# Transposing the residual's first half one weight part later, in a two-layer hybrid encoder step on one core

## The reference, cut to what matters

```
z = rmsnorm(h, ln_in) @ w_in                      # split: attention, gates, convolution
y_a = rmsnorm(o_a * silu(g_a), ln_out_a)          # 512 columns, from attention
y_c = rmsnorm(v * silu(g_c), ln_out_c)            # 512 columns, from the convolution
h = h + concatenate([y_a, y_c]) @ w_out           # (1024 x 1024)
gate = sigmoid(rmsnorm(h, ln_pg) @ w_pg)          # (1024 x 1024)
h = h + gate * (p @ w_pe)
```

## Time and profile before

| | us |
|---|---|
| median of 3 runs | 846.02 |
| lowest and highest | 844.46, 846.97 |
| the profiled execution, its time | 844.46 |
| the profiled execution, its span | 842.6 |
| PE busy in the span | 785.6 (93%) |
| DVE busy | 572.4 (68%) |
| ACT busy | 410.5 (49%) |

### The profile page before, as it was taken

How to read it: one execution, slowest core, us unless ns; L and a number is a source line. 1 busy time by engine, 2 the same in 40 slices (tenths; PEclk the granted TensorE clock), 3 DMA queues, 4 the chain that set the end, 5 groups by cost and what they waited for, 6 DMA issues and landing times.

```text
span 842.6 us, 10488 instructions
## 1 busy us (share of the span) xinstructions
PE 785.6 (93%) x3782; PEld 608.4 (72%) x3782; DVE 572.4 (68%) x1093; ACT 410.5 (49%) x944; POOL 67.9 (8%) x104
## 2 busy tenths in 40 slices
PE   6999999889998899999999999998999889999992
PEld 5789778547665568888888878774667556888881
DVE  3337968878894786555463688788899577656455
ACT  3655645544345573244365474555343547223544
POOL 5000123000000340000000012220000011000000
PEclk9999999989999999999999999999999999999996
DMA  9622222110000053412172223120000003342203
GB/s 298 186 71 76 70 66 79 35 51 4 22 26 1 25 184 111 154 63 90 51 263 66 75 70 89 46 69 26 26 26 25 1 1 106 133 137 75 76 1 124
DMA packets 40569, 65.26 MB, mean 77 GB/s; under 512 B 7774, under 2 KB 19898, under 8 KB 40502
## 3 DMA queue, kind: packets, MB, share of 16 engines
q1 hardware_dynamic: 37354, 58.45, 21.7%
q0 software_dynamic: 3104, 6.12, 2.5%
q10 hardware_dynamic: 60, 0.02, 0.0%
HBM read 57.86 MB, written 7.17 MB: 77 GB/s over the span
## 4 chain that ended last, share of the span: by engine, by line
PE 84%; ACT 8%; DVE 4%; issue 2%; DMA 1%; SPq 0%; DVEq 0%; ACTq 0%
PE acc L598 18%; PE acc L600 18%; PE acc L599 17%; PE sharedT L532 6%; PE sharedS L802 4%; PE acc L711 4%; PE sharedO L814 4%; PE sharedT L791 3%; ACT JUNK L928 2%; PE sharedT L785 2%; PE sharedO L532 1%; PE sharedS L532 1%; ACT WHI L932 1%; ACT KH L932 1%; PE sharedS L751 1%
## 5 line engine op out<-in xcount | busy, mean ns | idle before, releaser
L598 PE MATMUL acc<-WHI,XHI 128*128 128x512 f32 (+1 forms) x720 | 310.5, 431 | 3.0 <-DVE WLO L1285 2.3
L600 PE MATMUL acc<-WHI,XLO 128*128 128x512 f32 (+1 forms) x720 | 279.9, 389 | 0.0
L599 PE MATMUL acc<-WLO,XHI 128*128 128x512 f32 (+1 forms) x720 | 279.2, 388 | 0.0
L1349 DVE SCALAR_TENSOR_TENSOR VT<-UX,CWT,VT 128x640 f32<-128x640 f32 x240 | 211.9, 883 | 5.3
L1285 DVE SCALAR_TENSOR_TENSOR WLO<-WR,GT,WHI 128x512 fp32r<-128x512 f32 (+1 forms) x144 | 100.1, 737 | 103.9 <-ACT WHI L932 103.8
L598 PEld LDWEIGHTS acc<-WHI,XHI 128*128 128x128 f32 x720 | 136.4, 189 | 33.4 <-issue 6.0
L599 PEld LDWEIGHTS acc<-WLO,XHI 128*128 128x128 f32 x720 | 136.5, 190 | 28.9 <-issue 6.0
L600 PEld LDWEIGHTS acc<-WHI,XLO 128*128 128x128 f32 x720 | 135.8, 189 | 26.8
L932 ACT ACTIVATE WHI<-WR,GT 128x512 fp32r<-128x512 f32 (+1 forms) x144 | 94.8, 708 | 114.1 <-PE acc L600 108.7
L932 ACT ACTIVATE PT<-sharedT 128x384 f32<-128x384 f32 (+1 forms) x80 | 35.9, 449 | 76.3 <-PE sharedT L532 76.1
L814 PEld LDWEIGHTS sharedO<-V,PT 128*128 128x128 f32 x320 | 44.2, 191 | 19.6 <-issue 14.5
(11 more groups left out here) (191 smaller groups left out, 855.8 us busy)
## 6 DMA issues: line engine op xcount, KB each, us to landing
WR<-in_w_in_dram SPq DMA_DIRECT2D x32, 256.0 KB, 3.1
WR<-in_w_in_dram SPq DMA_DIRECT2D x16, 512.0 KB, 3.6
WR<-in_w_out_dram SPq DMA_DIRECT2D x16, 512.0 KB, 3.8
WR<-in_w_pg_dram SPq DMA_DIRECT2D x16, 512.0 KB, 3.5
WR<-in_w_in_dram SPq DMA_DIRECT2D x8, 416.0 KB, 3.4
residual_spill<-H SPq DMA_DIRECT2D x5, 512.0 KB, 3.4
H<-residual_spill SPq DMA_DIRECT2D x10, 256.0 KB, 3.2
H<-in_x_prompt_dram SPq DMA_DIRECT2D x4, 512.0 KB, 8.1
```

The costliest lines, as they stand in the source:

```text
L598: mm(out, hi, w_hi, start=(first and k == 0), stop=False)
L599: mm(out, hi, w_lo, start=False, stop=False)
L600: last = mm(out, lo, w_hi, start=False, stop=(final and k == 1))
L1349: ins = stt(out=out, in0=src, scalar=w, in1=out, op0=ALU.mult, op1=ALU.add)
```

## The change

In each of the two layers the five flips of `("h", t, 0)` on PE move from behind the quanta of part 0 of `oc1` to behind those of part 1. On DVE the five drains of `oc0` now stand together, followed by `low(27)` and then the five low halves in a row. ACT's order, SP's and POOL's are as before. No instruction is added or removed.

```diff
@@ -891,7 +891,7 @@
             for c in range(2):
                 for t in range(TILES):
                     quantum("oc1", c, t)
-                    if c == 0:
+                    if c == 1:
 
                         pe.wait_ge(acc_drained[t], BLK[l, "oc0"] + 1)
                         flip_half((l, ("h", t, 0)), H[:, t, :])
@@ -1551,12 +1551,9 @@
             low(first_i + 26)
             for t in range(TILES):
                 onto_residual("oc0", t)
-                if t == 3:
-                    low(first_i + 27)
-                if t > 1:
-                    low_half((l, ("h", t - 2, 0)))
-            low_half((l, ("h", 3, 0)))
-            low_half((l, ("h", 4, 0)))
+            low(first_i + 27)
+            for t in range(TILES):
+                low_half((l, ("h", t, 0)))
             low(first_i + 28)
             for t in range(TILES):
                 onto_residual("oc1", t)
```

## The result

| | us |
|---|---|
| before, median of 4 | 845.24 (842.53 to 846.97) |
| with the change, median of 4 | 857.99 (857.3 to 858.8) |
| ratio | 1.0154, 95% interval 1.0125 to 1.0184 |
| the profiled execution with the change, a fifth run | 859.08, span 857.3 |

The kernel is slower by 12.75 us at the medians, 1.5%. The profiled spans differ by 14.7 us, because the profiled execution of before lies under its median and that of after above its own. The prediction was 857.3 us.

A forecast was written before the change was run, and what follows sets the result against it. PE was taken to bound the kernel, with no gap at the change. Stalls of 8.5 us plus 2.8 for low clock made 11.3, added to the 846.02 median: 857.3 us, range 853.3 to 860.5.

The forecast's parts named there:

- points 1 and 4: Around `pg0` and DVE's `oc0` drains: PE's own work stays the same in sum, and the earlier drains bring 0.
- points 1 and 2: Behind layer 0's last flip: it starts 6.80 us later, at 364.14, and the serial ACT and DVE chain moves equally.
- point 3: Ahead of `pg0`: PE waits for the tile 0 drain of `oc1`, a stall of 4.25 us per layer.
- the 4.14 ahead of the 0.11: At `pg0`: 4.14 us later start (368.77 instead of 364.63), then 0.11 more lost at its second matmul.
- The bound by `low(28)` alone: At `pg0`: lower bound if the tile 0 drain weren't needed; PE goes at 368.10, 3.6 us per layer.
- point 5: Behind `pg0`: second flips add nothing, every engine follows PE, all is 4.25 us later and nothing returns the stall.
- point 7: PE's clock after the stall: falls to half rate in both layers, costing 1.4 us per layer, 2.8 in all.
- rival B: After the stall, in `pg0`: low clock lasts twice 3.4 us, losing 3.4 us per layer; time 861.3, chance 0.05.

The follow-up runs named there:

- the filled kernel: Against the kernel with the change: four unused float32 matmuls per layer on PE behind the last flip of the residual's first half; 852.85 us, ratio 1.0098.

## Why the prediction held

1. *PE bound, so nothing to gain* (points 1 and 4). It held: DVE's new order alone gave no gain, at the same mean clock it cost about 0.4 us, and PE has no wait there with or without it.
2. *The chain moves with the last flip by 6.80 us* (points 1 and 2). Worked out: `pg0` at 368.77. Measured: 370.31, less the 1.46 by which this execution was already late, 368.85.
3. *The stall is 4.25 us per layer, ended by the drain* (point 3). Measured 4.22 and 4.2, with DVE's drain named as the releaser. These are from start to start, so they answer to the 4.14 ahead of the 0.11. The difference of 0.08 is PE's start behind the drain, 0.14 (369.50 + 0.67 to 370.31) where I had taken 0.06 from a wait for a `low`; the loss at the second matmul was 0.08 where the clock was up (368.41 to 368.72 in the filled kernel, less 0.23). The bound by `low(28)` alone, 3.47 without the 0.11, came out at 3.5 (4.22 less the 0.7 that the drain was worth).
4. *Nothing gives it back* (point 5). It held: layer 0 alone cost 6.5 us. The first low half of `("h", t, 1)` came at 374.57, with DVE idle for 1.78 ahead of it, more room than the 0.1 us I had worked out, since PE was slow by then.
5. *The clock falls, worth 1.4 us per layer* (point 7). The mechanism was right and the size too small: 1.69 in layer 0 and 2.7 in layer 1 of the profiled execution, 3.7 to 4.7 in all by the experiment that filled the stall, against 2.8. I had put the low stretch partly into the stall. In layer 0 it began behind it and fell wholly on work; in layer 1 it lasted 6.9 us, twice the 3.4 of the earlier trace rows and longer than the 4.3 that I took from the run's start. That is near what rival B had for both layers (6.8 us low each). Against B I had said that the start of the run took only 4.3 us. That was misread: I counted from the first product, but the flips ahead of it are slow too. The four from 6.65 take 1.11 us, where four take 0.60 at the high level, so the slow pace lasts over 9 us there, with two gaps of 0.75 in it:

```profile
6.65 1.11 PE L532 MATMUL sharedT<-IDENT,H 128*128 128x128 f32 x4
```
6. *The sum.* 11.3 us predicted, 12.75 at the medians. That the median came so close (857.99 for 857.3) is partly luck: the cost was 1.45 more than predicted, and the base 0.8 less, since it was 846.02 when I predicted and 845.24 with one run more. In the profiled seams nearly all of the difference is the clock's term, 4.4 for 2.8.

The rule of the Trainium skill that I weighed (TensorE: Matmul & The Clock Gate, section "Why this matters for your kernels") came out as it says for the gaps of 3.4 and 4.1 us: the clock fell behind all five of them that were profiled. The rule warns of gaps longer than some microseconds, and shorter ones were not safe here: behind the gap of 2.2 us the clock fell in one layer and stayed up in the other, and in the attention stage of the kernel before it fell behind gaps of at most 1.9 us.

## What to carry to other kernels

When PE's work is reordered, look at what stands behind the moved item in the queues of the engines that serve it: each engine takes its instructions in order, so preparation for the next block waits with it even though it doesn't need it. With that preparation moved ahead of the item the reorder cost nothing here (ratio 1.0006); with it left behind, what remained of the chain came back as a stall of 4.2 us, once per layer. A stall of PE can have a second price in its clock. Where PE has to wait anyway, a few matmuls whose results nobody uses can keep the clock up: they gave 3.7 to 4.7 us back in the stall, and 4.7 us in the attention stage.

## What the runs showed that I had not expected

- The kernel before has time to gain from its clock: filling the waits of one seam per layer gave 4.7 us of 844 back, and took the mean clock to 0.993.
- The length of a low stretch varies: 3.4 us in layer 0 and 6.9 us in layer 1, behind waits of the same 4.1 us.
- The same wait of 2.2 us left the clock at 1.00 in one layer and brought it to 0.50 in the other.
- Most of the spread of the kernel before goes with its clock. On one chip it ran 23 times, from 840.14 to 847.03 us. The 13 runs with a mean granted clock of 0.987 or more have a median of 842.8, the nine with 0.981 or 0.982 one of 846.5. Together with the experiment that filled the attention stage (0.991 to 0.993, 838.92 to 842.05) this makes the clock the likely cause. What decides it from run to run stays open. A difference of 2 us between two kernels therefore means little until their mean clocks are compared.
